# Order of the recurrence's levels and of the weight rounding on ACT, POOL and VectorE, in a two-layer hybrid encoder on one NeuronCore

## What is computed

```python
xn = rms_norm(x, pre_norm[layer])
proj = xn @ w_in[layer]
(a_qkv, a_gate, b_q, b_k, b_v, b_gate,
 c_q, c_ff, c_fb, c_i, c_gate, merge) = jnp.split(proj, split_points, axis=-1)
ya = dilated_attention(...) * silu(a_gate)            # branch A, 12 heads
yb = banded_window_attention(..., sink) * silu(b_gate)  # branch B, 8 heads
yc = hgrn2_bidirectional(c_q, c_ff, c_fb, c_i, c_gate, lb, norm)  # branch C, 8 heads
g = sigmoid(merge).reshape(b, s, 3, D_MODEL)
y = g[:, :, 0] * (ya @ w_branch_a) + g[:, :, 1] * (yb @ w_branch_b) + g[:, :, 2] * (yc @ w_branch_c)
x = x + rms_norm(y @ w_out[layer], post_norm[layer])
```

## Time and profile before

| | |
|---|---|
| median of 3 runs | 2141.4 us (2141.28 to 2141.57) |
| the profiled execution | 2141.19 us, span of its instructions 2139.4 us |
| PE busy | 2128.5 us, 99% of the span, 11590 matmuls |
| DVE, ACT, POOL busy | 1553.3 us (73%), 1067.6 us (50%), 1247.9 us (58%) |
| ACT's rounding L487 | 366 times, mean 1917 ns |
| POOL's remainder L490 | 367 times, mean 2778 ns |
| DVE's remainder L490 | 371 times, mean 1638 ns |
| granted clock of TensorE | 0.999 |
| HBM | 188 GB/s over the span |

### The profile page before, as it was taken

One profiled execution on the slowest core, in us unless ns is written; L12 is line 12 of the kernel. 1 busy time (PEld: TensorE's weight loads), 2 busy tenths in 40 slices (PEclk: granted clock), 3 DMA queues, 4 the chain that ended last, 5 costly groups with the idle time before them and its releaser, 6 DMA issues.

```text
span 2139.4 us, 28844 instructions
## 1 busy us (share of the span) xinstructions
PE 2128.5 (99%) x11590; PEld 1766.3 (83%) x11590; DVE 1553.3 (73%) x2176; ACT 1067.6 (50%) x1048; POOL 1247.9 (58%) x583
## 2 busy tenths in 40 slices
PE   9999999999999999999999999999999999999998
PEld 8888888888888888888888888888888888888887
DVE  7982789898876886555388737898898767865653
ACT  6444444446666655434454434345466566544442
POOL 5455544336785867666544554444367857676664
PEclk9999999999999999999999999999999999999999
DMA  8555445455455454755565554453554554447554
GB/s 338 190 190 194 177 163 192 140 181 190 177 179 180 174 179 176 256 197 192 184 224 190 194 196 171 164 196 138 179 195 177 178 177 177 178 177 255 193 190 149
DMA packets 60404, 403.86 MB, mean 189 GB/s; under 512 B 7408, under 2 KB 7536, under 8 KB 12912
## 3 DMA queue, kind: packets, MB, share of 16 engines
q1 hardware_dynamic: 60128, 401.50, 52.2%
q10 hardware_dynamic: 144, 0.52, 0.1%
HBM read 397.80 MB, written 4.19 MB: 188 GB/s over the span
## 4 chain that ended last, share of the span: by engine, by line
PE 89%; POOL 4%; DVE 4%; ACT 2%; issue 1%; DVEq 0%; POOLq 0%; ACTq 0%
PE acc L1282 84%; PE side L1282 4%; POOL w_lo L490 2%; POOL arena L625 1%; DVE wide L962 1%; DVE w_lo L490 1%; POOL arena L622 1%; POOL arena L623 1%; ACT w_hi L487 1%; DVE arena L1107 0%; DVE arena L1095 0%; PE side L1448 0%; DVE arena L1081 0%; DVE arena L1085 0%; DVE aT_lo L1195 0%
## 5 line engine op out<-in xcount | busy, mean ns | idle before, releaser
L490 POOL TENSOR_TENSOR w_lo<-raw,w_hi 128x768 fp32r<-128x768 f32 x367 | 1019.5, 2778 | 847.6 <-ACT w_hi L487 836.5
L487 ACT ACTIVATE w_hi<-raw 128x2048 fp32r<-128x2048 f32 x366 | 701.3, 1917 | 823.8 <-PE acc L1282 808.2
L490 DVE TENSOR_TENSOR w_lo<-raw,w_hi 128x1280 fp32r<-128x1280 f32 (+1 forms) x371 | 607.3, 1638 | 505.1 <-ACT w_hi L487 502.0
L1282 PE MATMUL acc<-w_hi,xT_hi 128*128 128x512 f32 x2112 | 653.7, 392 | 0.1
L1282 PE MATMUL acc<-w_hi,xT_lo 128*128 128x512 f32 x2112 | 647.7, 389 | 0.0
L1282 PE MATMUL acc<-w_lo,xT_hi 128*128 128x512 f32 x2112 | 525.9, 391 | 0.0
L1282 PEld LDWEIGHTS acc<-w_hi,xT_lo 128*128 128x128 f32 x2112 | 396.4, 188 | 83.4 <-DVE xT_lo L451 0.2
L1282 PEld LDWEIGHTS acc<-w_lo,xT_hi 128*128 128x128 f32 x2112 | 393.9, 188 | 81.7
L1282 PEld LDWEIGHTS acc<-w_hi,xT_hi 128*128 128x128 f32 x2112 | 392.9, 188 | 79.3 <-issue 0.3
L962 DVE STREAM_TRANSPOSE arena<-stage 32x256 f32<-32x256 f32 (+1 forms) x480 | 204.7, 427 | 7.1
L1107 DVE TENSOR_TENSOR arena<-arena 128x512 f32<-128x512 f32 x64 | 84.5, 1320 | 31.5 <-ACT arena L862 31.5
(11 more groups left out here) (143 smaller groups left out, 1945.0 us busy)
## 6 DMA issues: line engine op xcount, KB each, us to landing
raw<-w_stream SPq DMA_DIRECT2D x366, 1024.0 KB, 4.8
x_out<-arena SPq DMA_DIRECT2D x16, 256.0 KB, 2.7
arena<-x_turned_in SPq DMA_DIRECT2D x4, 514.0 KB, 7.4
arena<-x_in SPq DMA_DIRECT2D x2, 1024.0 KB, 14.6
arena<-x_in SPq DMA_DIRECT2D x4, 512.0 KB, 5.7
wide<-post_in SPq DMA_DIRECT2D x2, 1024.0 KB, 7.3
arena<-x_out SPq DMA_DIRECT2D x4, 512.0 KB, 5.7
raw<-w_stream SPq DMA_DIRECT2D x3, 512.0 KB, 7.2
```

The lines of the kernel that those rows point to most:

```text
L487: return act.activation(w_hi[:, g % ROUNDED, :], raw[:, g % LANDING, :], ACT.Copy)
L490: return eng.tensor_tensor(w_lo[:, g % LANDING, cols], raw[:, g % LANDING, cols], w_hi[:, g % ROUNDED, cols].bitcast(F32), ALU.subtract)
L1282: return pe.matmul(out, a, b, start=start, stop=stop)
```

## The change

On ACT and POOL, the recurrence's level is moved from its place in the iteration to the front of it, ahead of the rounding or the remainder of tile s+2. On DVE the level is put in a function `level(u, l)`; for even l it is called at the front of the iteration, for odd l where it stood, behind the remainder and the preparations of the units. On ACT that puts the level ahead of the evacuations too. No instruction is added or removed, and no wait is changed: TensorE's and SP's programs are the same.

```diff
 POOL
                     for s in range(NSTEPS):
-                        g = layer * NSTEPS + s + 2
-                        if s < NSTEPS - 1 and g < TOTAL:
-                            lo(g)
-                        if s == 3:
...
                         for u in range(4):
                             l = s - REC[u] - FIRST_LEVEL
                             if 0 <= l < LEVELS - 1:
                                 pool.wait_ge(S.decays, LEVELS * u + l + 1)
...
                                 pool.tensor_tensor(grown, grown, crossed(PI, L, 511, l, step=0), ALU.add).then_inc(S.scanned, 1)
+                        g = layer * NSTEPS + s + 2
+                        if s < NSTEPS - 1 and g < TOTAL:
+                            lo(g)
+                        if s == 3:
...
 ACT
                     for s in range(3, NSTEPS):
+                        for u in range(4):
+                            l = s - REC[u] - FIRST_LEVEL
+                            if 0 <= l < LEVELS:
+                                if l == 0:
+                                    act.wait_ge(S.logs_ready, u + 1)
+                                else:
+                                    if l >= 2:
+                                        act.wait_ge(S.grams, (LEVELS + 1) * u + l - 1)
+                                    act.wait_ge(S.scanned, (LEVELS - 1) * u + l)
+                                n, L = 512 >> (l + 1), 1 << l
+                                act.activation(crossed(keys(l), 0, L, l), crossed(RX, 0, 512 + L, l), ACT.Exp, scale=-1.0)
+                                act.wait_ge(S.mixed, (LEVELS + 1) * u + l + 1)
+                                act.activation(crossed(EQ[:, 0], 0, L, l), crossed(PI, 0, 512 + L, l),
+                                               ACT.Exp).then_inc(S.decays, 1)
                         if s < NSTEPS - 1 and layer * NSTEPS + s + 2 < TOTAL:
                             hi(layer * NSTEPS + s + 2)
...
-                            l = d - FIRST_LEVEL
-                            if 0 <= l < LEVELS:
...
 DVE
+                def level(u, l):
+                    if 0 <= l < LEVELS:
+                        if l == 0 and u:
+                            dve.wait_ge(S.rec_out, u)
+                        if l >= 1:
+                            keep(u, l - 2)
+                        dve.wait_ge(S.decays, LEVELS * u + l + 1)
+                        dve.tensor_tensor(decayed_q(l), rec_views(u)[0], EQ[:, 0], ALU.mult).then_inc(S.mixed, 1)
+                        if l == LEVELS - 1:
+                            keep(u, l - 1)
...
                     for s in range(3, NSTEPS):
+                        for u in range(4):
+                            if (s - REC[u] - FIRST_LEVEL) % 2 == 0:
+                                level(u, s - REC[u] - FIRST_LEVEL)
                         if s < NSTEPS - 1 and layer * NSTEPS + s + 2 < TOTAL:
                             lo(layer * NSTEPS + s + 2)
...
-                            l = d - FIRST_LEVEL
-                            if 0 <= l < LEVELS:
...
+                            if (d - FIRST_LEVEL) % 2:
+                                level(u, d - FIRST_LEVEL)
```

More of the change, by code:

```diff
@@ L603, in _ @@
                             lo(1)
-                        g = layer * NSTEPS + s + 2
-                        if s < NSTEPS - 1 and g < TOTAL:
-                            lo(g)
-                        if s == 3:
-                            pool.wait_ge(S.x_squared, 2)
-                            link(power(x_rstd, x_sumsq, 1.0 / D))
-                            pool.tensor_scalar(half_rstd, x_rstd, 0.5, None, ALU.mult).then_inc(S.x_rstd_ready, 1)
                         for u in range(4):
@@ L625, in _ @@
                                 pool.tensor_tensor(grown, grown, crossed(PI, L, 511, l, step=0), ALU.add).then_inc(S.scanned, 1)
+                        g = layer * NSTEPS + s + 2
+                        if s < NSTEPS - 1 and g < TOTAL:
+                            lo(g)
+                        if s == 3:
+                            pool.wait_ge(S.x_squared, 2)
+                            link(power(x_rstd, x_sumsq, 1.0 / D))
+                            pool.tensor_scalar(half_rstd, x_rstd, 0.5, None, ALU.mult).then_inc(S.x_rstd_ready, 1)
+                        for u in range(4):
                             if s == REC[u] + FIRST_LEVEL + 9:
```

## The result

The changed kernel takes 2149.54 us, median of 5 executions (2148.85 to 2150.00), against 2141.4 us before (5 executions of the same session). The ratio is 1.0038, 95% interval 1.0027 to 1.0049. It is slower by 8.1 us, beyond the 4.3 us that I called distinguishable and outside the range of 2137.5 to 2147.0. The profiled execution took 2149.6 us.

What follows compares the result with a forecast made beforehand. TensorE, busy 99% of the span, was taken as the bound, so only its waits could be won, with POOL and DVE sharing SBUF beneath. -3.56 + 3.1 + 0.8 = +0.4 us gave 2141.6 us, range 2137.5 to 2147.0.

Steps and rivals of the forecast that it cites:

- (c): Last level of a unit: DVE's product of level 7 comes late for TensorE in units 2 and 3; +0.8 us, both layers.
- (b): ACT's levels ahead of its rounding: the z_a accumulator's evacuation holds TensorE at steps 104 and 119, both layers; +3.1 us.
- (a): Even levels ahead of the remainder on DVE: TensorE's three stalls per layer before a gram go; -3.56 us.
- The list for unit 1: Worked times for (b) at step 104: the evacuation ends at 617.65 and TensorE waits 0.96 us.
- enough for the same list: Step 109, which has level 7, lasts 6.55 us, so the evacuation makes no stall there.
- the three signs of being wrong: TensorE waits for a remainder or rounding anywhere; steps 104 and 119 stay at 5.44 us; any other step gains a wait.
- The slower rival: z_a's evacuation falls behind DVE's level 1 product, delayed by POOL's remainder; stalls 10.0 us, not 3.1; 2148.5 us; chance 0.15.
- (d): Remainders behind the level on POOL and DVE: covered by the two steps they run ahead; cost nothing.

## Why the prediction was wrong

**The step that failed is (c), the last level of a unit.** It was put at +0.8 us, with 0.3 for unit 3, 0.1 for unit 2 and nothing for unit 0. It measured +9.4 (1.9, 0.9 and 1.9 us in each layer, for units 0, 2 and 3) or +9.6 with unit 1. For unit 3 the chain was the right one. Step 132 began 2.94 us later than in my working; with that taken off, POOL ended level 6 at 822.2, inside my 819.4 to 822.5 but at its far end, where I had taken the near one. The near end took POOL for full; in the changed kernel it stood idle for 42.0 us before the first operation of a level, waiting for exponentials, against 17.1 us before. M(7) needed 6.8 us from there and not 5.8, because POOL's remainder, made ready by the same rounding, was ahead of it on the shared resource. I had applied that rule in (b) and left it out in (c). Unit 0 I had never worked out: its chain is DVE's own full queue, and so is unit 2's, which I had put at 0.1 without a list of its own. The run with M(7) alone ahead is 8.6 us faster than the changed kernel. In the sum, (c) came out 8.6 us above its term, (a) gave 1.2 us less than counted and (b) cost 1.9 us less, which together is the miss of 7.9 us.

**(a) was right in two places of three.** Steps 135 and 137 went to their floor, -2.3 us. Step 124 kept its wait (7.11 us): M(6) of unit 2 waits for DVE's transposes and keep (730.45 to 733.62), not for a remainder. That is 1.2 us less than counted. With all levels ahead it goes (6.55).

**(b) was too high.** The list for unit 1 ended 0.96 us past the edge, the measured evacuation at the edge: POOL's two operations of level 0 took 2.1 us and not 2.64, since M(0) waited for the first and not the first for it, which is half of the 1.0 us; the rest is in small gaps of the list. Cost 0.2 us in steps 105, none in 120. The 1.0 us of step 109 in the second layer I had excluded with "enough for the same list". Together 1.2 against 3.1. Two of the three signs of being wrong that I had named came: steps 104 and 119 kept their length, and steps 95, 105 and 109 gained waits.

**The slower rival** came out at 2148.5 us, within 1 us of the measured time, and by the wrong mechanism: the evacuation cost 1.2 us of the 10 that it had. M(1) did keep ahead of POOL's remainder (it asked at 613.90, the remainder at 614.24), as I had argued against this rival. It had 0.15; that its time was near is luck. The true mechanism, a late M(7), had no chance of its own. (d) was right: no remainder was late, the least time to spare was 4 us.

The same product took 1.68 us behind POOL's remainder and 0.68 us without it. The rule drawn on in (b) says so (the Trainium skill, SBUF — State Buffer, section Who interferes with whom): "Issue order, not op shape, decides who blocks." Here the trace agrees.

What is shown by runs: that M(7) behind the remainder costs the 8 us; that 1.1 us of each wait of units 0 and 3 is the shared resource; that the evacuation is 1.2 us; that the gain over the kernel before needs ACT's part, POOL's part and more of DVE's odd levels than the last (with M(7) alone ahead the ratio was 0.9997). What is argued from timelines alone: the full queue of DVE in units 0 and 2, the loop over the transposes in unit 2, and why level 6 behind its remainder costs as much as it does.

## What to carry to other kernels

When a step of a chain is moved ahead on two engines, move it ahead on the third as well, or list every wait of the chain again: a half move puts the third engine's other work inside the chain (here odd products behind a remainder, behind a rounding, behind the exponentials). Here the full move took 2139 us against 2141 before, and the partial moves tried took between 2141 and 2286 us. Work out the last link of each unit first, because lag collects there, and for every unit, not for the one that was tightest before. On a shared resource an earlier request is not always better: it may only let the other engine's long instruction in first.

## What the hardware showed that I had not expected

TensorE's clock fell in steps with a long wait, and not in each of them. Stretches of ACT's-level-7-behind-the-rounding run, in step 125 of the first layer, and last a stretch of the same step in the second (length, busy of the five engines, then the granted clock, which is 1.00 at 2.4 GHz and 0.50 at 1.2 GHz):

```profile
741.00:744.00 3.00, 0.97 (x5) 0.49 (x3) 2.97 (x5) 2.71 (x3) 0.09 (x1) 0.99 0.46 194
744.00:745.00 1.00, 1.00 (x5) 1.00 (x6) 1.00 (x2) 0.00 (x0) 1.00 (x1) 0.50 0.08 16
...
747.00:748.00 1.00, 1.00 (x5) 0.82 (x4) 0.80 (x1) 0.00 (x0) 0.00 (x0) 0.82 0.00 0
...
1814.00:1816.00 2.00, 1.85 (x12) 1.73 (x13) 2.00 (x3) 0.70 (x2) 1.82 (x1) 1.00 0.00 0
```

and TensorE's timeline at the two waits, of the first and of the second layer:

```profile
743.88 2.05 PE L1306 MATMUL side<-arena,wide 128*128 128x128 f32 x8 [2.03 <-DVE arena L1023]
745.59 2.92 PE L1306 MATMUL acc<-w_lo,bT_hi 128*128 128x512 f32 x8
...
1814.15 1.16 PE L1306 MATMUL side<-arena,wide 128*128 128x128 f32 x8 [2.02 <-DVE arena L1023]
```

In both layers TensorE was idle for 2.0 us ahead of the same gram. In the first the granted clock was 0.50 from 744 to about 747.4, the gram took 2.05 us and the eight matmuls after it 2.92; in the second it stayed at 1.00, and the gram took 1.16. That made 11.97 us of step 125 in one layer and 10.36 in the other: 1.6 us for a wait that was no longer. In the changed kernel itself, with waits up to 1.7 us, the granted clock is 1.00 in all these steps. The run with level 6 behind spreads over 2161 to 2168 us, the changed kernel over 1.2 us. Its mean granted clock goes with the time: 0.998 in the execution of 2161.1 us, 0.997 in that of 2163.4 and 0.995 in the two of 2167.7. That the clock is the whole of the spread is not shown.
